# A two-layer diffusion transformer: modulation units placed by need, accumulator zeros written earlier, four expert loads held until the tokens are there

## The reference

```python
for l in range(2):
    mod   = silu(c)     @ w_mod[l] + b_mod[l]        # 6 x 1024 values for latent tokens
    mod_c = silu(c_ctx) @ w_mod[l] + b_mod[l]        # and for context tokens
    sh_a, sc_a, gt_a, sh_f, sc_f, gt_f = split(mod, 6)
    h   = modulate(rms_norm(x), sh_a, sc_a)          # and hc of the context
    mix = token_mixers(h, hc, ...)                   # linear attention, neighbourhood and window attention
    x   = x + gt_a * rms_norm(mix @ w_out[l])
    h   = modulate(rms_norm(x), sh_f, sc_f)
    # expert choice: each of 16 experts takes its 64 best latent (32 best context) tokens
    x   = x + gt_f * rms_norm(expert_choice_ffn(h, w_router[l], w_gate[l], w_up[l], w_down[l]))
    # layer 0 updates the context tokens in the same way, layer 1 does not
return x
```

## Time and profile before

| what | us |
|---|---|
| median of 3 runs (2184.46 to 2189.82) | 2186.5 |
| the profiled execution, its own time | 2191.71 |
| span of that execution | 2189.9 |
| TensorE busy | 1920.4 |
| VectorE busy | 544.8 |
| ScalarE busy | 472.3 |
| GpSimd busy | 162.7 |

### The profile page before, as it was taken

The page is one execution under the profiler, slowest core; times in us unless marked ns, Lnnn a source line. Parts: engine busy times, 40 slices in busy tenths (PEclk is TensorE's granted clock), DMA queues, the critical chain, the costliest instruction groups (busy, mean ns, idle before and its releaser), DMA issues.

```text
span 2189.9 us, 25241 instructions
## 1 busy us (share of the span) xinstructions
PE 1920.4 (88%) x10460; PEld 895.2 (41%) x10460; DVE 544.8 (25%) x1164; ACT 472.3 (22%) x967; POOL 162.7 (7%) x230
## 2 busy tenths in 40 slices
PE   5998998999849999999998299879993998988885
PEld 3655554775423333333333155446741333332331
DVE  1021452672250000000000402346615011111113
ACT  4131112442311011110111513114412111110111
POOL 0000010110110101101011000011101000000000
PEclk9999999999969999999999599989996999999997
DMA  9111149301369999999997412000017999999994
GB/s 390 39 54 62 39 204 426 139 11 58 129 266 359 395 395 388 391 394 394 396 376 309 161 39 77 0 10 30 11 58 312 404 427 428 429 427 429 428 427 186
DMA packets 52750, 541.77 MB, mean 247 GB/s; under 512 B 6352, under 2 KB 8656, under 8 KB 23232
## 3 DMA queue, kind: packets, MB, share of 16 engines
q1 hardware_dynamic: 34400, 486.72, 53.9%
q0 software_dynamic: 18128, 53.95, 7.5%
q10 hardware_dynamic: 144, 0.01, 0.0%
HBM read 516.54 MB, written 24.12 MB: 247 GB/s over the span
## 4 chain that ended last, share of the span: by engine, by line
PE 71%; DMA 18%; DVE 6%; ACT 3%; issue 1%; POOL 0%; SPq 0%; PEldq 0%; PEld 0%; DVEq 0%; POOLq 0%; ACTq 0%
DMA ring<-in_wstream 17%; PE ps L1658 15%; PE ps L1337 9%; PE ps L1721 7%; PE ps L1558 6%; PE ps L1666 5%; PE ps L1315 5%; PE ps L1728 3%; PE ps L1505 3%; PE ps L1443 2%; PE ps L1307 1%; PE ps L1478 1%; PE ps L1258 1%; PE ps L1285 1%; PE ps L1471 1%
## 5 line engine op out<-in xcount | busy, mean ns | idle before, releaser
L1658 PE MATMUL ps<-ring,work 128*64 128x512 f32 x2048 | 464.6, 606 | 37.0 <-DMA ring<-in_wstream 32.6
L1658 PEld LDWEIGHTS ps<-ring,work 128*64 128x64 f32 x2048 | 145.5, 139 | 349.9 <-issue 290.2
L1721 PE MATMUL ps<-big,work 128*64 128x512 f32 x1024 | 237.1, 605 | 3.1 <-ACT work L710 3.1
L1187 DVE TENSOR_TENSOR work<-glao,ps 128x512 f32<-128x512 f32 x32 | 22.0, 687 | 831.9 <-ACT glao L716 440.1
L1337 PE MATMUL ps<-hT,ring 128*128 128x512 f32 (+1 forms) x592 | 206.4, 507 | 1.9 <-DVE hT L856 1.4
L1337 PEld LDWEIGHTS ps<-hT,ring 128*128 128x128 f32 x592 | 112.2, 190 | 95.0 <-issue 86.4
L1558 PE MATMUL ps<-ring,hT 128*128 128x512 f32 x320 | 138.7, 592 | 0.0
L1721 PEld LDWEIGHTS ps<-big,work 128*64 128x64 f32 x1024 | 68.3, 138 | 140.3 <-issue 131.2
L1666 PE MATMUL ps<-ring,work 128*32 128x512 f32 x1024 | 119.8, 597 | 0.0
L1315 PE MATMUL ps<-ring,hT 128*128 128x384 f32 (+3 forms) x384 | 110.9, 450 | 0.0
L632 ACT ACTIVATE work<-ps,work 128x512 f32<-128x512 f32 (+2 forms) x120 | 81.9, 684 | 62.3 <-DVE work L996 31.5
(11 more groups left out here) (253 smaller groups left out, 2004.5 us busy)
## 6 DMA issues: line engine op xcount, KB each, us to landing
ring<-in_wstream SPq DMA_DIRECT2D x166, 2048.0 KB, 14.3
big<-in_wstream SPq DMA_DIRECT2D x64, 2048.0 KB, 13.3
x_kept<-big POOLq DMA_DIRECT2D x14, 512.0 KB, 2.9
big<-x_kept POOLq DMA_DIRECT2D x14, 512.0 KB, 6.8
xn_lat<-big POOLq DMA_DIRECT2D x8, 512.0 KB, 16.2
big<-in_x_all SPq DMA_DIRECT2D x6, 512.0 KB, 6.5
work<-in_nat_bias POOLq DMA_DIRECT2D x16, 192.0 KB, 2.7
big<-in_x_all POOLq DMA_DIRECT2D x6, 512.0 KB, 6.3
```

The source lines that it names most:

```text
L1658: last = T.matmul(bank(m)[64 * h:64 * h + 64, :], XST[:, kc, e, 0:CAP_L], gate_up[j][:, kk, m * D + h * 512:m * D + (h + 1) * 512], start= ...
L1721: last = T.matmul(bank(3)[64 * g:64 * g + 64, :], HT[:, kc, 0:CAP_L], down[j][:, kc % 4, h * 512:(h + 1) * 512], start=kc == 0, stop=kc == ...
```

## The change

- **Modulation units by need.** One unit in each of the 12 context pairs: 4 to 9 (the rest that layer 0 needs up to its route) and 16 to 21 of layer 1. Four units (10 to 13) go into the route of layer 0, between logits and picked tokens; two (14, 15) behind the experts of layer 0; two (22, 23) into the route of layer 1. The stream is ordered anew to match, and the ring slots of an expert's first four units turn by `FFN_TURN`. TensorE no longer drains after a unit: SP waits on the semaphore of `mod_rows`.
- **Zeros.** GpSimd clears a tile of `work` at the start, and writes the six DMAs of zeros when the first unit of input projections of layer 0 is done. VectorE waits for them before it clears its own states there.
- **Held loads.** In layer 0 the first expert's units 2 to 5 wait until the first pair's tokens have landed. In layer 1 the order of the six first loads is 0, 1, 4, 5, 2, 3.
- **Passage.** Behind the experts of layer 0 each load waits for its own slot; two modulation units come ahead of the five IN units.

```diff
+MOD_ATT = [4, 5, 6, 7, 8, 9, 16, 17, 18, 19, 20, 21]
+MOD_ROUTE = [[10, 11, 12, 13], [22, 23]]
+MOD_BOUND = [14, 15]
+FFN_TURN = [FFN_AT[0] % RING, (FFN_AT[1] - FFN_UNITS) % RING]
+FIRST_LOADS = [[0, 1, 2, 3, 4, 5], [0, 1, 4, 5, 2, 3]]
...
@@ SyncE
+            def used(n):
+                if n in mod_units:
+                    sp.wait_ge(sem("modrow"), mod_place(mod_units[n]))
+                else:
+                    sp.wait_ge(ring_used[lap(n)[0]], sum(...))
...
-                for j in range(SLOTS):
+                for j in FIRST_LOADS[l]:
+                    if l == 0 and j == 2:
+                        sp.wait_ge(sem("xs_rows"), fetched(l, 1))
                     if j < RING:
-                        n = max(n for n in range(last - RING + 1, last + 1) if lap(n)[0] == j)
-                        sp.wait_ge(ring_used[j], lap(n)[1] + 1)
-                    elif j == RING:
+                        s = (j + FFN_TURN[l]) % RING
+                        n = max(n for n in range(last - RING + 1, last + 1) if lap(n)[0] == s)
+                        used(n)
+                    elif j == SLOTS - 2:
                         sp.wait_ge(sem("x_saved"), 16 * [NT, NT + NLT][l])
...
-                    for n in range(IN_AT[1], FFN_AT[1]):
-                        if n < IN_AT[1] + RING:
-                            sp.wait_ge(ffn_used[lap(n)[0]], NE)
-                        sp.wait_ge(ring_used[lap(n)[0]], lap(n)[1])
+                    for n in range(FFN_AT[0] + FFN_UNITS, FFN_AT[1]):
+                        if n < FFN_AT[0] + FFN_UNITS + RING:
+                            sp.wait_ge(ffn_used[(lap(n)[0] - FFN_TURN[l]) % RING], NE)
+                        else:
+                            used(n - RING)
                         load(n)
@@ GpSimd
+            zero = w(8 * TOK, D)
+            pool.memset(zero, 0.0).then_inc(sem("acc_zero"), 1)
+            pool.wait_ge(sem("acc_zero"), 1)
+            pool.wait_ge(sem("proj"), n_items(0, 1))
+            for t in range(NLT): pool.dma_start(acc_lat[...], zero).then_inc(sem("added"), 16)
+            for t in range(NCT): pool.dma_start(acc_ctx[...], zero).then_inc(sem("added"), 16)
...
-                if l < DEPTH - 1:
-                    zero = ACC[:, 0, :]
-                    pool.memset(zero, 0.0).then_inc(sem("acc_zero"), 1)
-                    ... the same six DMAs
-                else:
+                if l == DEPTH - 1:
@@ ScalarE
-            def modrow(n):
-                act.wait_ge(sem("modrow"), n + 1)
-                S.activation(MODROW, bank(2), ACT.Copy).then_inc(sem("modrow_out"), 1)
+            def modrow(n, row, src):
+                act.wait_ge(sem("modrow"), mod_place(n))
+                S.activation(row, src, ACT.Copy).then_inc(sem("modrow_out"), 1)
...
+                for n in MOD_ROUTE[l]:          # route, behind the exponential of the logits
+                    modrow(n, SGL, bank(0))
+                if l < DEPTH - 1:               # behind gate_rows(l, "f")
+                    for n in MOD_BOUND:
+                        modrow(n, SGL, bank(0))
@@ VectorE
+                if l == 0:                      # gla_state
+                    dve.wait_ge(sem("added"), ZERO_DMAS)
...
+                for g in ((3, 4), (6,))[l]:     # route, behind the copies of VALS
+                    mod_out(g, bank(1))
+                if l < DEPTH - 1:               # behind gate_rows(l, "f")
+                    mod_out(5, bank(1))
+                    dve.wait_ge(sem("mod_out"), 6)
@@ TensorE
                 last.then_inc(sem("modrow"), 1)
-                pe.drain().then_inc(ring_used[lap(at)[0]], 1)
...
-                def mods(p, k): ...
+                def mods(p):
+                    if l == 0 and 1 <= p <= CTX_PAIRS:
+                        if MOD_ATT[p - 1] == 16:
+                            pe.wait_ge(sem("mod_out"), 2)
+                        mod_cols(MOD_ATT[p - 1], MODROW, bank(5))
+                    if l == 0 and p < CTX_PAIRS:
+                        mod_rows(MOD_ATT[p], bank(2))
...
                 last.then_inc(sem("logits"), 1)
+                mods = MOD_ROUTE[l]
+                mod_rows(mods[0], bank(0))
                 pe.wait_ge(sem("aff"), 1 + l * PER["aff"])
...
                 last.then_inc(sem("affT"), 1)
+                for k, n in enumerate(mods):
+                    mod_cols(n, SGL, bank(1))
+                    if k + 1 < len(mods):
+                        mod_rows(mods[k + 1], bank(0))
...
                 gate_rows(l, "f")
+                if ctx_too:
+                    for n in MOD_BOUND:
+                        mod_rows(n, bank(0))
+                        mod_cols(n, SGL, bank(1))
```

More of the change, by code:

```diff
@@ L34, with mod_place @@
 MOD_EARLY = 4
-IN_AT = [MOD_EARLY, 2 * MOD_UNITS + IN_UNITS + OUT_UNITS + FFN_UNITS]
-OUT_AT = [2 * MOD_UNITS + IN_UNITS, IN_AT[1] + IN_UNITS]
-FFN_AT = [OUT_AT[0] + OUT_UNITS, OUT_AT[1] + OUT_UNITS]
+CTX_PAIRS = NCT * (NAT_H + SWA_H) // 2
+MOD_ATT = [4, 5, 6, 7, 8, 9, 16, 17, 18, 19, 20, 21]
+MOD_ROUTE = [[10, 11, 12, 13], [22, 23]]
+MOD_BOUND = [14, 15]
+MOD_ORDER = list(range(MOD_EARLY)) + MOD_ATT + MOD_ROUTE[0] + MOD_BOUND + MOD_ROUTE[1]
+MOD_GROUPS = [(0, 4), (4, 10), (16, 22), (10, 12), (12, 14), (14, 16), (22, 24)]
+IN_AT = [MOD_EARLY, 0]
+OUT_AT = [IN_AT[0] + IN_UNITS + len(MOD_ATT), 0]
+FFN_AT = [OUT_AT[0] + OUT_UNITS + len(MOD_ROUTE[0]), 0]
+IN_AT[1] = FFN_AT[0] + FFN_UNITS + len(MOD_BOUND)
+OUT_AT[1] = IN_AT[1] + IN_UNITS
+FFN_AT[1] = OUT_AT[1] + OUT_UNITS + len(MOD_ROUTE[1])
 N_UNITS = FFN_AT[1] + FFN_UNITS
+FFN_TURN = [FFN_AT[0] % RING, (FFN_AT[1] - FFN_UNITS) % RING]
+FIRST_LOADS = [[0, 1, 2, 3, 4, 5], [0, 1, 4, 5, 2, 3]]
 def mod_at(n):
[L43 to L50, removed]
+    if n < MOD_EARLY:
+        return n
+    if n in MOD_ATT:
+        return IN_AT[0] + IN_UNITS + MOD_ATT.index(n)
+    if n in MOD_BOUND:
+        return FFN_AT[0] + FFN_UNITS + MOD_BOUND.index(n)
+    l = 0 if n in MOD_ROUTE[0] else 1
+    return OUT_AT[l] + OUT_UNITS + MOD_ROUTE[l].index(n)
+def mod_place(n):
+    return MOD_ORDER.index(n) + 1
 def lap(n):
@@ L246, in __call__, with ffn_slot @@
                 self.eng.wait_ge(self.sem, self.n)
+        def ffn_slot(l, j):
+            return slot[(j + FFN_TURN[l]) % RING if j < RING else j]
         def width(l):
@@ L337, in bass_hybrid_dit, with fetched @@
         COMB_BANKS, LAST_BANKS = (7, 0, 1), (0, 1, 2)
+        def fetched(l, i):
+            return 32 * i if l < DEPTH - 1 else 16 * i + 32 * PAIRS * (DEPTH - 1)
         block = ctx.enter_context(nc.Block())
@@ L346, in load @@
                 sp.dma_start(ringv[:, p, :], wstream[n, :, :]).then_inc(ring_full[p], 16)
[L348 to L358, removed]
-                    sp.wait_ge(ring_used[lap(n)[0]], lap(n)[1])
-                    load(n)
+            def used(n):
+                if n in mod_units:
+                    sp.wait_ge(sem("modrow"), mod_place(mod_units[n]))
+                else:
+                    sp.wait_ge(ring_used[lap(n)[0]], sum(lap(m)[0] == lap(n)[0] and m not in mod_units for m in ring_units if m <= n))
+            mod_units = {mod_at(k): k for k in range(2 * MOD_UNITS)}
+            ring_units = list(range(FFN_AT[0])) + list(range(FFN_AT[0] + FFN_UNITS, FFN_AT[1]))
             for t in range(NT):
@@ L399, in _ @@
             pool.memset(ones[:, :], 1.0).then_inc(sem("ones_set"), 1)
+            zero = w(8 * TOK, D)
+            pool.memset(zero, 0.0).then_inc(sem("acc_zero"), 1)
+            pool.wait_ge(sem("acc_zero"), 1)
+            pool.wait_ge(sem("proj"), n_items(0, 1))
+            for t in range(NLT):
+                pool.dma_start(acc_lat[2 * P * t:2 * P * (t + 1), :].rearrange("(p h) c -> p (h c)", h=2), zero).then_inc(sem("added"), 16)
+            for t in range(NCT):
+                pool.dma_start(acc_ctx[4 * P * t:4 * P * (t + 1), :].rearrange("(p h) c -> p (h c)", h=4), zero).then_inc(sem("added"), 16)
             for l in range(DEPTH):
@@ L651, in attend @@
                     if l == 0 and p < CTX_PAIRS:
-                        for n in MOD_STEP[p]:
-                            modrow(n)
+                        modrow(MOD_ATT[p], MODROW, bank(2))
                     if p == pairs(l):
@@ L1056, in gate_rows @@
                 s = 0 if half == "a" else 1
+                if half == "f":
+                    dve.wait_ge(sem("mod_out"), (5, 7)[l])
                 for wch in range(2 if l < DEPTH - 1 else 1):
@@ L1608, in ffn @@
                 per = 2 * nt
-                gate_up = [v3(slot[j], 2) for j in range(4)]
+                gate_up = [v3(ffn_slot(l, j), 2) for j in range(4)]
                 down = [v3(slot[4 + j], 4) for j in range(2)]
```

52 lines of the change are left out of this document (19 added, 33 removed).

## The result

The changed kernel takes 2162.86 us (median of 4 runs, 2158.92 to 2164.66), the kernel before 2188.06 beside it (4 runs): ratio 0.9889, 95% interval 0.9869 to 0.9908. That is 25 us less; 28.6 were forecast.

| stretch | before | after | difference |
|---|---|---|---|
| start to the last modulation columns of the attention | 388.59 | 362.48 | -26.1 |
| from there to the transposes of the route, layer 0 | 210.32 | 210.29 | 0.0 |
| route of layer 0, up to the first expert | 48.31 | 48.96 | +0.7 |
| experts of layer 0 (to gate_rows) | 548.48 | 547.93 | -0.6 |
| passage (gate_rows to the first projection of layer 1) | 59.22 | 61.24 | +2.0 |

What follows compares the result with a forecast made beforehand. TensorE's own order, with hand-overs to ScalarE and VectorE, was taken to pace the context pairs. Terms -27.5 + 0.9 - 2.5 + 0.5 = -28.6 us, applied to the median 2186.5, gave 2158 us; range 2149 to 2171.

Steps and rivals of the forecast that it cites:

- Attention, -27.5: Layer 0's context pairs: 8 units fewer, steps of 5.55 us instead of 7.60, last columns at 360.8 instead of 388.59.
- C: Context pairs: the step is longer, 18.6 us gained instead of 27.5, time 2167; chance 0.07.
- D: Context pairs don't speed up, their chain of maxima, exponentials and transposes needs 7.6 us; time 2186, chance 0.03.
- Zeros, nothing: Clearing and six DMAs moved from the route to the projections, where queues are free: nothing either way.
- Route, +0.9: Route of layer 0: rows of unit 10 cost 0.5 us, VectorE's two bias additions 0.4; range 0.3 to 6.
- rival A: Route 0 pays: modulation at half clock, the four held loads served side by side; 2167, chance 0.09.
- Held loads, nothing: First expert of layer 0: the hold costs nothing, loads land in turn with 9 us or more cover.
- Passage, -2.5: Between layer 0's experts and layer 1: early loads use the DMA gap, two later ones share with the additions; 2.5 us less.
- rival B: The passage loses: the two late loads delay the last additions, 2163.5 us; chance 0.10.
- Layer 1, +0.5: Route and start of layer 1: rows of unit 22 cost 0.3 us, one bias addition 0.2.
- Rival E: Layer 0's additions take longer per expert beside SP's never-empty queue; at 36.3 us each, time 2192; chance 0.05.

Runs made afterwards that it cites:

- half_rows: Changed kernel with only four of the eight `mod_rows` products for each of the 12 attention units: 2155.48 us, ratio 0.9864 to the kernel before.
- drain: Changed kernel with TensorE draining again behind each of the 12 modulation units of the attention: 2164.83 us, ratio 0.9906 to the kernel before.
- mix_first: Changed kernel with VectorE taking away pair p-4's output ahead of pair p-2's transposes in the context pairs: 2153.06 us, ratio 0.9863 to the kernel before.
- hold_in: Changed kernel with layer 1's third and fourth IN loads waiting until layer 0's last additions landed: 2157.69 us, ratio 0.9877 to the kernel before.
- zeros_back: Changed kernel with the zeros written in the route again, the hold kept: 2158.98 us, ratio 0.9879 to the kernel before.
- slot3_first: Changed kernel with the first load behind layer 0's experts waiting for the fourth slot again, so four issue at once: 2168.97 us, ratio 0.9922 to the kernel before.
- both: Changed kernel with `x_again` split around the last additions and the two later IN loads held until these landed: 2156.85 us, ratio 0.9857 to the kernel before.
- hold_reads: Changed kernel with `x_again` split around the last additions and two later IN loads held until the accumulators were read: 2146.11 us, ratio 0.9822 to the kernel before.
- no_hold: Changed kernel without the wait for tokens before the first expert's units 2 to 5 in layer 0: 2169.86 us, ratio 0.9928 to the kernel before.

## Why the prediction held, and where it did not

The time (2162.9 against 2158, range 2149 to 2171) and the sign were right. By its steps:

- **Attention, -27.5:** -26.1 in the profile. The mechanism was right: the step is 5.45 us (5.55 forecast), and that TensorE's order sets the pace is shown by half_rows, drain and mix_first: each moves the step by what it adds or takes (-0.85, +0.29, -0.74). Rivals C and D, a longer or an unchanged step, are out, though the stretch gained only 18.0 us, near C's 18.6: that came from the wait and the clock below, not from longer steps throughout. That the sum came so close is luck. It ran from the first scores to the last columns, 60.4 us, and the profile has 70.3 there. It left out TensorE's wait of 2.49 us for ScalarE at the start and took too little for the half clock, which the steps behind that wait had (20.6 us for the first three instead of 13.2) and two later ones as well; the granted clock was 0.83 in the stretch against 0.97 before. The 8.15 us that the first scores came earlier, which no step of the prediction counted, made up for most of it. Where that wait was short, the stretch took 59.8 us (hold_in) and 61.4 (zeros_back), near the forecast.
- **Zeros, nothing:** right with the hold (zeros_back). In the new order without hold they would cost 5.9 us, which the step did not look at.
- **Route, +0.9:** +0.7, but not by its terms. I had taken 0.5 for the rows of unit 10 and 0.4 for the bias additions; from the last products of the logits to the affinities it is 3.41 us (3.51 before) and from the indices to the tokens 7.80 (7.74 before), so neither cost anything to speak of. What made the route longer are the transposes ahead of the logits (1.1 us more). The modulation ran at full clock: rival A is out.
- **Held loads, nothing:** right against the kernel before, wrong in what it was for. I had read from the old trace that the loads land before the fetch, and carried that over to an order in which they are issued later. The hold is worth 8.5 us of the 25.
- **Passage, -2.5:** +2.0. This step failed, and rival B was nearer the truth. The early loads did use the gap, worth 8 us of passage (slot3_first), and the two behind them were issued when forecast (5.6 and 9.2 us behind the start of `gate_rows`; 5.7 and 9.2 forecast). The term that was mis-sized is how long the additions take beside these two: I had given the transfers of GpSimd half of the DMA rate, so that the additions land 17 us behind the last products, or 25 if the loads were served first. It was 23.6 (22.0 before), a loss of 1.5 us instead of a gain of 4.5. The reads behind, for which I had added 2 us, took 3.63 us against 3.52. The Trainium skill (DMA: Bandwidth & Descriptors, Queues, rings and completion order) has the DMA engines take turns between queues packet by packet. I had taken that as even shares of bytes, which the page does not say; the trace is nearer to the other bound. Why the shares are uneven stays open.
- **Layer 1, +0.5:** 0.0 in its route. The 2.5 us gained in its projections and attention, where both kernels run the same code, belong to no step; all thirteen profiles of the changed kernel and its variants have that code and give 390.8 to 393.8 us for the stretch, so the 394.7 of the one profile before stands alone, and what of it is chance is open.
- **Rival E** did not occur: the experts of layer 0 kept 34.2 us each.

## What to carry to other kernels

Work taken from a full stage is paid for where it lands: here the attention gained 18 us in its own stretch (18 to 28 in the profiles with the same attention code), 14 would have been lost in the route, and only the held loads kept them. A forecast that comes out right should be checked term by term: two terms here were off by 8 to 10 us each and cancelled. When loads are placed anew, do not read their landing times from the old trace: ask what each must wait for now, and which short transfer on the critical path it will meet. A hold must reach past the last of these transfers; ended one step early it only moved the collision (hold_in, both), ended behind the reads, and with `x_again` split, it took 13 us off the passage (hold_reads).

## What the runs showed of the hardware that I had not expected

- Additions of one expert, issued behind 3.1 MB of GpSimd's own transfers, landed 8.6 us after issue when no weight loads ran beside them, 17.5 us with two loads of 2.1 MB issued just after, and 25.8 us where four more loads had been issued together some 17 us before.
- The indirect fetch (0.8 MB in two DMAs) landed 4.3 us after the issue of its second DMA when the loads were held, 12.7 us with six weight loads issued before it, and 18.6 us with 3.1 MB of zeros in its own queue as well.
- The same attention code had a mean granted clock of 0.83, 0.90 and 0.96 over the context pairs in three profiles (changed kernel, no_hold, hold_in), and 70.3, 66.0 and 59.8 us from its first scores to its last columns. The two lower ones had waited 2.5 us for ScalarE before their first columns and fell to the half level behind that wait; hold_in had waited 0.25 us and did not.
